# Hybrid decoder trunk: gate and up weights of the experts in four parts of 2 MB with 4 KB rows, in place of two of 4 MB with 8 KB rows

## The reference, cut to what matters

```python
for g in range(MOE_GROUPS):                       # 4 groups of 8 experts, D = 1024, F = 256
    hid = (jax.nn.silu(jnp.einsum('nd,edf->nef', t, w_gate_e[g]))
           * jnp.einsum('nd,edf->nef', t, w_up_e[g]))
    hid = hid * combine[:, g, :, None].astype(hid.dtype)
    out = out + jnp.einsum('nef,efd->nd', hid, w_down_e[g]).astype(F32)
```

## Time and profile before

| what | value |
|---|---|
| median of three runs | 1659.34 us |
| the profiled execution's own time | 1660.32 us |
| span in its profile, first to last instruction | 1658.5 us |
| mean granted clock of TensorE | 0.95 |
| PE busy | 1485.3 us (90%) |
| bytes moved by DMA | 349.59 MB |
| gate and up loads | 32 of 4096 KB |
| down loads | 32 of 2048 KB |

### The profile page before, as it was taken

The page is one execution under the profiler, slowest core; times in us unless marked ns, Lnnn a source line. Parts: engine busy times, 40 slices in busy tenths (PEclk is TensorE's granted clock), DMA queues, the critical chain, the costliest instruction groups (busy, mean ns, idle before and its releaser), DMA issues.

```text
span 1658.5 us, 19588 instructions
## 1 busy us (share of the span) xinstructions
PE 1485.3 (90%) x7988; PEld 1015.8 (61%) x7988; DVE 512.0 (31%) x1221; ACT 334.9 (20%) x640; POOL 65.3 (4%) x60
## 2 busy tenths in 40 slices
PE   7999999999999876777699999999999998776785
PEld 5885668887657554344268856688877574442441
DVE  3473457302101231121135634572021022311122
ACT  2222537200012010100022224462000120100010
POOL 0000310000000000000000013100000000000000
PEclk9999999999999977889999999999999998888897
DMA  8344222327340739999964332223274407499996
GB/s 299 134 153 152 102 102 102 106 102 279 128 153 23 279 136 417 393 419 416 392 223 148 133 127 102 102 102 106 102 279 152 152 2 306 191 405 419 417 418 262
DMA packets 115673, 349.59 MB, mean 211 GB/s; under 512 B 11664, under 2 KB 13968, under 8 KB 99216
## 3 DMA queue, kind: packets, MB, share of 16 engines
q1 hardware_dynamic: 114912, 345.95, 54.3%
q0 software_dynamic: 688, 2.62, 0.4%
HBM read 347.50 MB, written 1.05 MB: 210 GB/s over the span
## 4 chain that ended last, share of the span: by engine, by line
PE 74%; issue 15%; DMA 7%; DVE 2%; ACT 1%; DVEq 0%; SPq 0%; POOL 0%; POOLq 0%
PE bank L670 27%; PE bank L652 23%; PE bank L844 7%; DMA ga<-in_w_down_e 6%; PE bank L629 3%; PE bank L922 2%; PE bank L942 2%; PE bank L782 2%; DMA wring<-in_w_up_e 1%; PE bank L971 1%; PE bank L883 1%; PE bank L771 1%; PE bank L897 1%; PE bank L807 1%; PE bank L827 1%
## 5 line engine op out<-in xcount | busy, mean ns | idle before, releaser
L670 PE MATMUL bank<-hT,wring 128*128 128x256 f32 x1536 | 337.6, 380 | 1.2 <-issue 1.2
L670 PEld LDWEIGHTS bank<-hT,wring 128*128 128x128 f32 x1536 | 289.7, 190 | 44.0 <-issue 4.9
L652 PE MATMUL bank<-wring,hT 128*128 128x512 f32 (+2 forms) x576 | 217.5, 534 | 0.0
L942 PE MATMUL bank<-wring,big 128*32 128x256 f32 x2048 | 141.5, 441 | 62.3 <-DMA wring<-in_w_up_e 45.9
L652 PEld LDWEIGHTS bank<-wring,hT 128*128 128x128 f32 x576 | 104.4, 191 | 105.3 <-issue 103.3
L942 PEld LDWEIGHTS bank<-wring,big 128*32 128x32 f32 x2048 | 72.6, 126 | 131.3 <-DMA wring<-in_w_up_e 49.7
L844 PE MATMUL bank<-big,wring 128*128 128x256 f32 x512 | 111.0, 379 | 2.0 <-ACT big L1045 2.0
L844 PEld LDWEIGHTS bank<-big,wring 128*128 128x128 f32 x512 | 97.1, 190 | 15.6 <-issue 2.5
L922 PE MATMUL bank<-big,xn 128*128 128x256 f32 x256 | 79.7, 483 | 23.1 <-DVE big L1576 23.1
L922 PEld LDWEIGHTS bank<-big,xn 128*128 128x128 f32 x256 | 70.2, 335 | 35.5 <-DVE big L1576 28.4
L1287 DVE SCALAR_TENSOR_TENSOR scr<-bank,prm,scr 128x255 f32<-128x255 f32 (+1 forms) x144 | 62.7, 477 | 58.6 <-ACT scr L1013 55.9
(11 more groups left out here) (228 smaller groups left out, 1404.1 us busy)
## 6 DMA issues: line engine op xcount, KB each, us to landing
wring<-in_w_in SPq DMA_DIRECT2D x68, 1024.0 KB, 7.0
wring<-in_w_gate_e SPq DMA_DIRECT2D x16, 4096.0 KB, 20.0
wring<-in_w_up_e SPq DMA_DIRECT2D x16, 4096.0 KB, 21.7
wring<-in_w_ssd_o SPq DMA_DIRECT2D x16, 1024.0 KB, 6.2
xs<-in_w_down_e SPq DMA_DIRECT2D x8, 2048.0 KB, 25.9
wring<-in_w_ckv SPq DMA_DIRECT2D x16, 1024.0 KB, 7.2
scr<-in_w_down_e SPq DMA_DIRECT2D x8, 2048.0 KB, 30.3
ga<-in_w_down_e SPq DMA_DIRECT2D x8, 2048.0 KB, 30.7
```

The source lines that it names most:

```text
L652: ins = nc.tensor.matmul(bank[job % 8][:, 0:width], src[:, k, t * P:(t + 1) * P], wring[:, SLOT[c], k, 0:width], start=i == 0, stop=i == K ...
L670: ins = nc.tensor.matmul(bank[job % 8][:, i * SEQ:(i + 1) * SEQ], wring[:, SLOT[c], k, m:m + P], src[:, k, :], start=n == 0, stop=n == KC - 1)
L942: ins = nc.tensor.matmul(bank[b][j * S:(j + 1) * S, i * F:(i + 1) * F], xg[:, k, e:e + S], up_part[i][:, j, k * F:(k + 1) * F], start=k == ...
```

## The change

The ring is used in four parts, one for each slot. Parts 0 and 1 hold the gate matrices of a block's four experts, parts 2 and 3 the up matrices; an even part has the first half of the contraction, an odd part the second. A partition's row of 8 KB in memory is cut into two pieces of 4 KB, one for each part, so that a load of 2 MB takes every second 4 KB of its block. The matmuls, their operands' values and their order stay as they were; PE waits for four loads in a block in place of two, and counts `gu_s` up four times. The waits on the ring in SP follow the parts: each part of the first pass waits for its own slot's last chunk, and each of the first four chunks of the next layer for its own part.

```diff
--- before.py
+++ after.py
@@ -188,7 +188,8 @@
 S = 32
 BE = 4
 NB = E // BE
-PARTS = 2
+PARTS = 4
+KH = KC // 2
 ROUNDS = SEQ // S
 GATHER = (6, 7, 4, 5)
 
@@ -325,8 +326,7 @@
         spare = hT[:, :, :].rearrange("p (t c) s -> p t (c s)", t=TT)
         cbm = cols(qiT[:, :, :].rearrange("p a b -> p (a b)"), 0, TT, SG * P)
 
-        up_part = [wring[:, 2 * i:2 * i + 2, :, :].rearrange("p (w j) k n -> p w j (k n)", w=1).rearrange("p w j (h m) -> p w (j h) m", h=2)[:, 0]
-                   for i in range(PARTS)]
+        up_part = [wring[:, i, :, :].rearrange("p (j h) n -> p j (h n)", j=BE) for i in range(PARTS)]
         xn_eighth = xn[:, :, :].rearrange("p t (q c) -> p t c q", c=KC)
         drows = [xs[:, :, :].rearrange("p t (a n) -> p (t a) n", a=2), scr[:, :].rearrange("p (j n) -> p j n", j=BE),
                  qq[:, :, :].rearrange("p t (a n) -> p (t a) n", a=2), ga[:, :].rearrange("p (j n) -> p j n", j=BE)]
@@ -481,7 +481,7 @@
                 kind = st[0]
 
                 if c < W_SLOTS:
-                    sp.wait_ge(gu_s, before * (PARTS * NB) + (SLOT[c] // 2 + 1))
+                    sp.wait_ge(gu_s, before * (PARTS * NB) + (SLOT[c] + 1))
                 else:
                     filled(sp, l, last_job(c - W_SLOTS))
                 settle(sp)
@@ -527,11 +527,11 @@
                 for b in range(NB):
                     for i in range(PARTS):
 
-                        filled(sp, l, last_job(NCH - W_SLOTS + 2 * i + 1))
+                        filled(sp, l, last_job(NCH - W_SLOTS + i))
                         settle(sp)
                         sp.wait_ge(gu_s, u * (PARTS * NB) + (PARTS * b + i + 1))
                         settle(sp)
-                        src = (w_gate, w_up)[i][l, g, b * BE:(b + 1) * BE].rearrange("j (p k) n -> p j (k n)", p=P)
+                        src = (w_gate, w_up)[i // 2][l, g, b * BE:(b + 1) * BE].rearrange("j (p h k) n -> h p j (k n)", p=P, h=2)[i % 2]
                         sp.dma_start(up_part[i][:, :, :], src).then_inc(up_part_in[i], 16)
                     for i in range(2):
                         if (b, i) not in down_ahead:
@@ -932,15 +932,17 @@
                 for b in range(NB):
                     for i in range(PARTS):
                         pe.wait_ge(up_part_in[i], (u * NB + (b + 1)) * 16)
-                        for k in range(KC):
-                            if b == 0 and i == 0 and k % 4 == 0:
-
-                                pe.wait_ge(xgv_rdy, u * 2 + (k // 4 + 1))
-                                pe.wait_ge(xga_rdy, u * 2 + (k // 4 + 1))
+                        w, half = divmod(i, 2)
+                        if b == 0 and w == 0:
+
+                            pe.wait_ge(xgv_rdy, u * 2 + (half + 1))
+                            pe.wait_ge(xga_rdy, u * 2 + (half + 1))
+                        for k in range(half * KH, (half + 1) * KH):
                             for j in range(BE):
                                 e = (b * BE + j) * S
-                                ins = nc.tensor.matmul(bank[b][j * S:(j + 1) * S, i * F:(i + 1) * F], xg[:, k, e:e + S],
-                                                       up_part[i][:, j, k * F:(k + 1) * F], start=k == 0, stop=k == KC - 1)
+                                ins = nc.tensor.matmul(bank[b][j * S:(j + 1) * S, w * F:(w + 1) * F], xg[:, k, e:e + S],
+                                                       up_part[i][:, j, k % KH * F:(k % KH + 1) * F],
+                                                       start=k == 0, stop=k == KC - 1)
                         ins.then_inc(gu_s, 1)
                     pe.wait_ge(hid_s, u * NB + (b + 1))
                     for k in range(2):
```

## The result

The change made the kernel slower by about 3 us: 1662.62 us, the median of 20 runs (1657.51 to 1665.7), against 1659.47 us for the kernel before (20 runs, 1655.46 to 1661.48). The ratio is 1.0019, with a 95% interval of 1.0012 to 1.0026. The time lies in the forecast's range and within 0.3% of 1658.0 us, but it moved the other way: 1.3 us faster was forecast. The profiled execution took 1661.38 us, 1.2 us less than the median.

What follows compares the result with a forecast made beforehand. Expert loads were taken as bound by bytes and queue rate, apart from two dry places. Release -3.6, hole -3.8 and rows +6.1 sum to -1.3 us, against the 1659.34 us median: 1658.0 us, range 1650 to 1666 us.

Steps and rivals of the forecast that it cites:

- What bounds the kernel: Expert loads of both layers: bytes and queue rate alone set the time, 417 GB/s from 672 to 820 us.
- Earlier release ahead of the first pass: Start of each layer's expert loads, queue dry: gate's first quarter reloads 1.78 us sooner, 3.6 us gained over two layers.
- The hole: Second pass of each layer, queue briefly dry before block 1's gate load: it closes, 2.6 + 1.2 = 3.8 us gained.
- so 3.0 us of the 6.05 us go: PE's work on block 1's up: its first half, landed sooner, is done when the second lands, saving 3.0 us.
- Rows of 4 KB: Gate and up loads in both bound stretches: 411 GB/s in place of 420, 6.1 us lost.
- two rivals on rows: Bound gate and up loads: rows free, 420 GB/s, 1651.9 us, chance 0.19; or 388 GB/s, 1675.0 us, chance 0.13.
- The end: Behind each layer's last down load: the work that follows is untouched, so 0 us.
- The third rival, no earlier release: SP still held in an issue when the first half is free: no gains, +6.1 us, 1665.4 us, chance 0.08.

Runs made afterwards that it cites:

- the pair of 2 MB runs: Kernel before with each gate and up load issued as two 2 MB loads, coarse waits kept: 8 KB rows 1659.07 us, 4 KB rows 1667.96 us.

## Why the prediction was wrong

**What bounds the kernel:** right. The stretch is bound by bytes, and more so after the change: 214.1 to 214.2 us in layer 0 in three executions, where before it varied by over 1 us with the hole.

**Earlier release ahead of the first pass, -3.6 us:** right. The issue comes 3.5 us sooner over both layers in every execution; with the release alone, in the first pass only, 2.3 us of it were left at the end (0.3 to 4.1).

**The hole, -3.8 us:** it closes, but for somewhat less and partly by another way. One execution was read, with the largest hole of three in layer 0; by the windows of the three executions (366, 389 and 391 GB/s for 20 us, 384, 360 and 380 for 15 us, in place of about 415) the kernel before loses about 3 us to both holes in the mean. The step "so 3.0 us of the 6.05 us go" is too large: from the landing of up, or of its second half, to the end of the scatter it takes 13.7 us in the mean of three executions in place of 15.5, so 1.9 us go. Next late behind up's second half is the down load of the first rows, which lands about 5 us later whatever PE does, and PE waits for it in two of the three. In the changed kernel the hole closes all the same, since the next part is released by halves as well (659.73 us, 2.2 us after the pass's first gate matmul at 657.54 us); the run in which PE waits for both halves loses next to nothing there either. With the finer release and wait in the first pass only, layer 0 kept a hole.

**Rows of 4 KB, +6.1 us:** the mechanism was right and its size a little low. I took 411 GB/s from the down windows. The bound stretch after has 25.17 MB in 61.45 us, 409.5 GB/s, and 1.0 us more for a pass than before. A layer loads 3.5 passes' worth of gate and up there, so two layers pay 1.0 x 3.5 x 2 = 7 us; the run with coarse release gives 5 to 9 us by its interval. Of the two rivals on rows neither came: they are not free, and at 409 they are far from 388.

**The end, 0 us:** wrong, and the largest of the three errors: this is the step that failed. "The last load is a down load as before, and what follows it is untouched" holds for the instructions and not for their clock. PE now does half a matrix as each half lands, is done sooner, and idles for 2.7 to 3.2 us ahead of the last down load in five of six cases, where before it was at most 1.1; in these five the clock is at 1.2 GHz when the path comes back to PE. That costs 2.0 us behind layer 0 and 1.0 us behind layer 1 in the mean. Both runs that take the idle time away, one by a coarser wait and one by filler, bring the groups back to 1.92 and 3.89 us. That is shown in the traces; the whole times of these two runs lie too close to the changed kernel's to show it. The prediction had named the clock as an error of 2 us either way, at the start of layer 1, and had not asked what the change does to PE's idle time ahead of the last load.

The corrected sum: -3.5 (release) - 3 (hole) + 7 (rows) + 3 (tails) = +3.5 us, against 3.1 us measured (2.0 to 4.3 by the interval). Without the tails it would be +0.5 us. It is built in part from the runs that it explains, so that it comes so near is partly luck: hole and rows together are +4.7 us in the table, not +4, and the router's and gather's stretches are 2.3 us shorter there without a known cause.

**The third rival, no earlier release:** no. The issue came early in all executions, though SP now stands in full-queue issues more often.

**Left open.** The stretch from the norm's transposes to the first gate matmul was 1.5 and 0.8 us shorter after the change in the mean of three. It holds the same instructions and scatters by over 4 us in the changed kernel alone; whether the change has a share in it these runs don't tell. No run shows the tails' 3 us in the whole time either. The loads were also not tried as single loads of 4 MB with 4 KB rows, so the rows' price rests on the pair of 2 MB runs.

## What to carry to other kernels

In a stretch that is bound by bytes, a finer buffer is worth only what it starts earlier and the holes that it closes; if it shortens the rows of every load it is paid for on every byte, here 2.6% of the time per byte for 4 KB in place of 8 KB. Split the loads where the queue is dry and leave the others whole: that made this kernel 0.28% faster (0.15 to 0.42%), where splitting all of them made it 0.19% slower. And when PE's work is made to finish earlier ahead of a wait that stays, look at the clock it will have when the wait ends.

## What the runs showed of the hardware

The queue's rate steps with the row length and not with the number of loads: 420 GB/s with 8 KB rows (as 4 MB or as 2 MB loads), 409 to 412 with 4 KB rows (side by side in memory or every second one), 388 with 2 KB rows. The small-descriptor section of the Trainium skill's page "DMA: Bandwidth & Descriptors" has a fixed cost for each packet; an estimate from it gives 1.2% for the first step, and the runs show 2.6%. Ahead of the last load, 2.7 to 3.2 us of PE's idle time went with a last down group at a granted clock of 0.50 to 0.64, and at most 1.4 us with one at 1.00, in all runs. The length of one idle time alone does not decide it: in the second execution of the changed kernel the second half of up in layer 0's first pass ran at full clock (1.93 us) after 3.18 us.
